# A feed-forward block with seven half-size products in place of eight, its weight sums split between GpSimd and adding transfers

## The reference, cut to what matters

```python
def gated_conv_ffn(x, w_gate, w_up, conv_w, conv_b, w_down):
    g = jnp.einsum('bsd,df->bsf', x, w_gate)
    g = causal_dwconv3(g, conv_w) + conv_b
    up = jnp.einsum('bsd,df->bsf', x, w_up)
    return jnp.einsum('bsf,fd->bsd', jax.nn.silu(g) * up, w_down)
# x = rms_norm(h, norm_ffn[layer]), in both layers; all in float32
```

## Time and profile before

| | us |
|---|---|
| three runs | 1753.5, 1754.58, 1755.64 (median 1754.58) |
| the profiled execution, from first to last instruction (span) | 1753.3 |
| PE busy | 1722.9 (98%) |
| DVE busy | 955.8 (55%) |
| ACT busy | 776.2 (44%) |
| POOL busy | 406.6 (23%) |
| chain that ended last, share of PE | 82% |

### The profile page before, as it was taken

The page is one execution under the profiler, slowest core; times in us unless marked ns, Lnnn a source line. Parts: engine busy times, 40 slices in busy tenths (PEclk is TensorE's granted clock), DMA queues, the critical chain, the costliest instruction groups (busy, mean ns, idle before and its releaser), DMA issues.

```text
span 1753.3 us, 25674 instructions
## 1 busy us (share of the span) xinstructions
PE 1722.9 (98%) x8611; PEld 1438.5 (82%) x8611; DVE 955.8 (55%) x1757; ACT 776.2 (44%) x1375; POOL 406.6 (23%) x545
## 2 busy tenths in 40 slices
PE   7999999999999999999999999999999999999998
PEld 7788889999878888888888888888788788888887
DVE  5677867777763334675555555333346555555332
ACT  6666766666652223432443333322364433333222
POOL 4555665655520001000211111011003211111000
PEclk9999999999999999999999999999999999999999
DMA  4112123333323334223233333333232333333332
GB/s 137 52 45 63 42 59 79 81 74 87 75 67 96 96 108 133 61 85 101 84 108 93 94 93 95 120 95 94 96 96 72 87 94 96 96 96 93 93 96 91
DMA packets 284314, 154.42 MB, mean 88 GB/s; under 512 B 12655, under 2 KB 278770, under 8 KB 284242
## 3 DMA queue, kind: packets, MB, share of 16 engines
q1 hardware_dynamic: 281714, 148.69, 29.4%
q0 software_dynamic: 2336, 4.47, 1.1%
q10 hardware_dynamic: 192, 0.33, 0.1%
HBM read 147.02 MB, written 2.16 MB: 85 GB/s over the span
## 4 chain that ended last, share of the span: by engine, by line
PE 82%; DVE 8%; issue 4%; ACT 4%; POOL 1%; DMA 0%; ACTq 0%; DVEq 0%; SPq 0%; POOLq 0%
PE ps L364 65%; PE ps L980 3%; PE ps L2505 2%; PE ps L830 2%; DVE tmp L1323 1%; DVE arena_r L1328 1%; PE ps L843 1%; PE ps L809 1%; ACT tmp L1051 1%; PE ps L788 1%; PE ps L1773 1%; ACT w_split L305 1%; PE ps L347 1%; PE ps L676 1%; DVE tmp L1380 1%
## 5 line engine op out<-in xcount | busy, mean ns | idle before, releaser
L364 PE MATMUL ps<-u,w_split 128*128 128x512 f32 x3705 | 876.9, 394 | 0.0
L364 PEld LDWEIGHTS ps<-u,w_split 128*128 128x128 f32 x3705 | 690.8, 188 | 152.1 <-issue 1.4
L321 DVE TENSOR_TENSOR w_split<-w_raw,w_split 128x1024 fp32r<-128x1024 f32 (+1 forms) x221 | 268.2, 1214 | 434.3 <-ACT w_split L305 434.2
L305 ACT CAST w_split<-w_raw 128x1024 fp32r<-128x1024 f32 (+4 forms) x321 | 289.0, 914 | 412.3 <-PE ps L364 376.6
L364 PE MATMUL ps<-arena_r,w_split 128*128 128x512 f32 x1758 | 402.0, 389 | 1.8 <-POOL w_split L319 1.5
L364 PEld LDWEIGHTS ps<-arena_r,w_split 128*128 128x128 f32 x1758 | 329.5, 188 | 72.2 <-POOL w_split L319 1.9
L2425 POOL TENSOR_TENSOR tmp<-tmp 128x512 f32<-128x512 f32 x44 | 57.1, 1298 | 422.1 <-ACT tmp L2410 422.1
L319 POOL TENSOR_TENSOR w_split<-w_raw,w_split 128x256 fp32r<-128x256 f32 x168 | 122.9, 763 | 23.7 <-ACT w_split L305 23.7
L980 PE MATMUL ps<-u,w_split 128*128 128x264 f32 x768 | 105.8, 287 | 2.0 <-DVE arena_r L1348 1.8
L1921 POOL TENSOR_TENSOR tmp<-tmp 128x512 f32<-128x512 f32 x33 | 46.8, 1417 | 261.1 <-ACT tmp L1877 232.4
L1051 ACT ACTIVATE tmp<-ps,stats 128x144 f32<-128x144 f32 (+3 forms) x128 | 69.4, 542 | 75.1 <-DVE stats L1315 73.0
(11 more groups left out here) (283 smaller groups left out, 1701.1 us busy)
## 6 DMA issues: line engine op xcount, KB each, us to landing
w_raw<-in_w_in_dram SPq DMA_DIRECT2D x118, 256.0 KB, 3.1
w_raw<-in_w_ffn_gate_dram SPq DMA_DIRECT2D x88, 256.0 KB, 3.1
w_raw<-in_w_ffn_up_dram SPq DMA_DIRECT2D x88, 256.0 KB, 3.2
w_raw<-in_w_ffn_down_dram SPq DMA_DIRECT2D x64, 256.0 KB, 3.1
w_raw<-in_w_in_even_dram SPq DMA_DIRECT2D x32, 256.0 KB, 3.0
w_raw<-in_w_in_odd_dram SPq DMA_DIRECT2D x32, 256.0 KB, 3.1
w_raw<-in_w_ffn_down_dram SPq DMA_DIRECT2D x32, 192.0 KB, 2.7
w_raw<-in_w_br_mla_dram SPq DMA_DIRECT2D x16, 256.0 KB, 3.1
```

The lines of the kernel that those rows point to most:

```text
L305: ins = act.copy(dst, src)
L321: ins = eng.tensor_tensor(lo, r, hi, ALU.subtract)
L364: last = pe.matmul(out_ap, w_tile(c, ws, k - n0), moving(k, ms), start=start and n == 0, stop=stop and n == len(total) - 1, skip_group_che ...
```

## The change

The first two tiles of each FFN (`PLAIN = 2`) are made as before. For each of the other 20 tiles the pair `gate`, `up` is seen as one product of 2 x 2 blocks: the weights are g1, g2, u1, u2 (the even and the odd k-tiles of the gate panel and of the up panel; a "quarter" of 128 x 512 each), the input is B11, B12, B21, B22 (even or odd k-tiles, left or right 256 tokens). A scheme of the Strassen-Winograd kind needs seven products of 4 k-tiles x 3 passes x 256 columns in place of eight. It takes sums of weights, sums of inputs and sums of results:

- Weight sums, for every tile: `e = u1 + u2` (first, a POOL instruction), `u1 += g1` (third, a transfer from SBUF to SBUF with `accum_op=ALU.add`, which POOL begins), `g1 += e` (second, a POOL instruction, in place), `g2 += g1` (fourth, again an adding transfer).
- Low splits: of the seven weights of a tile the low parts of p5 and p7 are made by POOL (`POOL_LO`), the other five by DVE. ACT makes all seven high parts.
- Input: once a layer `x_tok` (the input with its gain and `rbc`) by DVE, four sums by POOL, seven high parts by ACT, seven low parts by DVE. The factor `rbc` disappears from the 20 tiles.
- Results: ACT copies the running sum out of PSUM three times a tile (`snap`), DVE adds three halves of 256 columns. Tap, silu and the product with `up` work on 512 columns as before, now partly in PSUM.

The products of one period stand in the order p1, p4, p3, p2, p6, p5, p7, where p4 and p3 belong to the tile of the period before (`OF_LAST`). High and low splits are made three products ahead, into four slots of a quarter each. Outside the FFN the diff renames semaphores (`pro_act` and the like) and moves the spatial weights' load, with no other change.

```diff
+SEVEN = ("p1", "p4", "p3", "p2", "p6", "p5", "p7")
+OF_LAST = (1, 2)
+POOL_LO = (5, 6)
+WEIGHT_OF = {"p1": "g1", "p2": "g2", "p3": "g2", "p4": "u2", "p5": "e", "p6": "g1", "p7": "u1"}
...
+        def pe_seventh(pe, layer, i, fs, pos):
+            kind, gs = SEVEN[pos], pair_of(fs, pos)
+            low_split(pe, layer, i, fs, pos)
...
+            elif kind in ("p4", "p3"):
+                out_ = bank(R_BANK + gs % 2, 0, HT) if kind == "p4" else bank(Q_BANK, 0, HT)
+                pe.wait_ge(sem("combined"), combined(layer, i, gs, "up_right"))
...
+            for kk in range(4):
+                for n, (ws, ms) in enumerate(PASSES):
+                    ins = pe.matmul(out_, split_slot(layer, fs, pos, ws)[:, kk * P:(kk + 1) * P], XS[kind][:, kk, ms, :],
...
+            ins.then_inc(sem("s_used"), 1)
...
+        def act_seventh(act, layer, i, fs, pos):
...
+            if kind in ("p1", "p2", "p4"):
+                loaded(act, layer, i, gs)
+            else:
+                if kind in ("p5", "p6"):
+                    act.wait_ge(sem("summed_w"), summed_to(layer, i, gs, 1 if kind == "p5" else 2))
+                else:
+                    act.wait_ge(sem("third_sum" if kind == "p7" else "fourth_sum"), added_to(layer, i, gs))
...
+            act.copy(split_slot(layer, fs, pos, HI), quarter(layer, gs, WEIGHT_OF[kind])).then_inc(sem("s_hi"), 1)
...
+            def first_sum(i, gs):
+                loaded(pool, layer, i, gs)
...
+                pool.tensor_tensor(quarter(layer, gs, "e"), quarter(layer, gs, "u1"), quarter(layer, gs, "u2"), ALU.add) \
+                    .then_inc(sem("summed_w"), 1)
+
+            def third_sum(i, gs):
+                pool.wait_ge(sem("summed_w"), summed_to(layer, i, gs, 1))
+                pool.dma_start(quarter(layer, gs, "u1"), quarter(layer, gs, "g1"), accum_op=ALU.add) \
+                    .then_inc(sem("third_sum"), 16)
+
+            def second_sum(i, gs):
+                low_split(pool, layer, i, gs, 0)
+                pool.wait_ge(sem("third_sum"), added_to(layer, i, gs))
+                dst = quarter(layer, gs, "g1")
+                pool.tensor_tensor(dst, dst, quarter(layer, gs, "e"), ALU.add).then_inc(sem("summed_w"), 1)
+
+            def fourth_sum(i, gs):
+                low_split(pool, layer, i, gs, 3)
+                pool.wait_ge(sem("summed_w"), summed_to(layer, i, gs, 2))
+                pool.dma_start(quarter(layer, gs, "g2"), quarter(layer, gs, "g1"), accum_op=ALU.add) \
+                    .then_inc(sem("fourth_sum"), 16)
...
+            def period(i, fs):
+                for pos in POOL_LO:
+                    seventh_low(pool, layer, i, fs, pos)
+                fourth_sum(i, fs)
+                if fs < FT - 1:
+                    first_sum(i, fs + 1)
+                    third_sum(i, fs + 1)
+                    second_sum(i, fs + 1)
```

The period of ACT (`begun`: the tile is one of the 20; `carried`: there is a tile before it):

```diff
+                if carried:
+                    snap(i, fs - 1, 3)
...
+                    hi_ahead(i, fs, 0)
...
+                    snap(i, fs, 1)
...
+                    hi_ahead(i, fs, 1)
+                    hi_ahead(i, fs, 2)
...
+                    hi_ahead(i, fs, 3)
...
+                    first_tap(i, fs - 1)
...
+                    hi_ahead(i, fs, 4)
+                    snap(i, fs, 2)
...
+                    pair_silu(i, fs - 1)
...
+                    hi_ahead(i, fs, 5)
+                    hi_ahead(i, fs, 6)
...
+                    hidden_hi(i, fs - 1)
```

And where the down product's first panels are loaded:

```diff
+            sp.wait_ge(sem("fourth_sum"), added_to(layer, 0, FT - 1))
...
+            w_load(sp, c0, panel(dram, 0, DOWN[0], 0))
+            low_split(sp, layer, 0, FT, 1)
+            low_split(sp, layer, 0, FT, 2)
+            w_load(sp, c0 + 1, panel(dram, 0, DOWN[1], DOWN[0]))
```

More of the change, by code:

```diff
@@ L203, in hybrid_blocks_kernel @@
         hid, at = view(tmp, at, 1, SEQ)
+        rbc_ffn, at = view(tmp, at, 1, SEQ)
         cpad, at = view(tmp, rest, 1, 516)
@@ L1838, in body @@
             def body(i, first, last):
+                if first and name in (("down", 0), ("down", 1)):
+                    down_first(sp, name[1], dram)
                 for j in range(2):
@@ new lines, in per_tile, with used, loaded, low_split @@
+        def per_tile(layer, i, fs, back=0):
+            return num(FT * layer + fs + 1 - back, i, 4)
+        def used(layer, i, fs, pos):
+            return num(N_PROD * layer + NTH[fs, pos] + 1, i, 28)
+        def loaded(eng, layer, i, gs):
+            eng.wait_ge(sem(f"pair_load{gs % 2}"), num(64 * (N_PAIR // 2 * layer + (gs - PLAIN) // 2 + 1), i, 128))
+        def low_split(eng, layer, i, fs, pos):
+            mine = [a_ for a_ in ORDER if (a_[1] in POOL_LO) == (pos in POOL_LO)]
+            per = sum((p in POOL_LO) == (pos in POOL_LO) for p in range(7))
+            eng.wait_ge(sem("s_lo_pool" if pos in POOL_LO else "s_lo"),
+                        num(len(mine) * layer + mine.index((fs, pos)) + 1, i, 4 * per))
@@ L2358, in load_ffn @@
         def load_ffn(sp, layer):
             c0 = FIRST[("ffn", layer)]
-            def body(i, first, last):
-                for j in range(4):
-                    w = a["w_ffn_gate_2" if j % 2 == 0 else "w_ffn_up_2"][layer]
-                    w_load(sp, c0 + j, panel(w, (2 * i + j // 2) * P), i, 4)
-            loop(sp, FT // 2, body)
+            for f in range(PLAIN):
+                for j in range(2):
+                    w_load(sp, c0 + 2 * f + j, panel(a["w_ffn_up_2" if j else "w_ffn_gate_2"][layer], f * P))
@@ L2419, in pool_ffn, with at_tile @@
+            periods(act, period)
+        def at_tile(eng, i, gs):
+            return gs if isinstance(i, int) else 4 * i + gs
         def pool_ffn(pool, layer, tag):
             pool.wait_ge(sem("rbc"), norms_done(tag))
-            def body(i, first, last):
-                for j in range(2):
-                    pool.wait_ge(sem("ffn_silu"), FT * layer + 2 * i + j + 1)
-                    pool.tensor_tensor(cnv[:, j, :], cnv[:, j, :], rbc[:, 0, :], ALU.mult) \
-                        .then_inc(sem("ffn_scaled"), 1)
@@ L2429, in dve_ffn, with period @@
+            scaled(1)
+            pool_x(pool, layer, 2)
+            pool_x(pool, layer, 3)
+            def period(i, fs):
+                for pos in POOL_LO:
[5 more added lines that the diff above has]
+                    second_sum(i, fs + 1)
+            for fs in range(PLAIN, FT):
+                period(0, fs)
         def dve_ffn(dve, layer, tag):
```

607 lines of the change are left out of this document (455 added, 152 removed).

## The result

The changed kernel takes **1839.07 us** (median of 4 runs, 1838.01 to 1839.96) against 1755.11 (1753.5 to 1756.17) for the kernel before on the same chip: ratio 1.0475, 95% interval [1.046, 1.049]. Two terms of the sum were wrong in opposite directions, so that it came so close is luck; most of what follows is about these two.

What follows compares the result with a forecast made beforehand. POOL's chain of sums, splits and transfers was taken to bound the FFN at 12.8 us a period, above PE's 10.1. Span 1753.3 + 70 (periods) + 23 (FFN starts and ends) = 1846.7, median 1848 us; range 1757 to 1945.

Steps and rivals of the forecast that it cites:

- PE's side: FFN period on PE: 84 matmuls of 0.120 us, 10.1 us instead of 11.04, saving 37 us if PE stays the bound.
- The ring of POOL: POOL's sums, low parts and hops each FFN period: 7.48 + T + 0.3 = 12.8 us, +70 us.
- T: Time from an adding transfer's issue to its landing, estimated at 3.04 + 0.9 + 1.1 = 5.0 us.
- ring A: POOL's cycle through the third sum's transfer, second sum, low parts, fourth sum's issue and first sum; forecast 12.8 us.
- The second ring: From the fourth sum's issue through p3's high part, third snap, p4, p3 and p7's splits: T + 7.4 us.
- Contention in the ring: POOL's additions stretched where they meet DVE's work on SBUF: 0.3 us a period, bounds 0 and 0.6.
- The stall: PE idle some 2.7 us a period before p4, waiting for DVE's `combined`, with little before p6.
- The boundaries: PE waits at each FFN's start (9 us) and before the down product (2.5): 11.5 a layer, +23 us.
- The end: Before the down product PE waits some 2.5 us, its first panel being loaded only after the last fourth sum.
- Rival 2: Adding transfers land fast, 2.6 us, and PE stays the FFN's bound: 1741 us; chance 0.07.
- Rival 3: Adding transfers much slower than copies, landing in 6.5 to 9.4 us: 1948 at 7.5, 2024 at 9.4; chance 0.09.
- Rival 4: PE's clock falls in the stalls, p4 and p3 taking 5.8 us in place of 2.9: 1948 us; chance 0.07.

Runs made afterwards that it cites:

- lodve_snap_rbanks: Changed kernel with the low parts of p5 and p7 moved from POOL to DVE, third snap earlier, four PSUM banks for R products: 1785.74 us, ratio 1.0175.
- both_pool: Changed kernel with the third and fourth weight sums as POOL additions in place of adding transfers: 1838.22 us, ratio 1.0468.
- no_xsums: Changed kernel without POOL's four sums of the input blocks, plain blocks split in their place: 1826.89 us, ratio 1.041.
- copies: Changed kernel with its two adding transfers made plain copies of the same size, leaving out the third and fourth sums: 1791.4 us, ratio 1.0203.
- both_rbanks: Changed kernel with both transfers replaced by POOL additions and four PSUM banks in place of two for R products: 1866.65 us, ratio 1.0652.

## Why the prediction was right, point by point

- **PE's side** was right. The fastest single periods, in `lodve_snap_rbanks`, are 10.02 us long (10.1 forecast). The 37 us of PE time were there, but no version held that period: the best mean is 10.54.
- **The ring of POOL** was right in its mechanism. With the measured T of 3.8 its formula, 7.48 + T + 0.3, gives 11.6; ring A closes in about 11.5. The second ring, T + 7.4 with its own T of 4.7, gives 12.1; measured 11.9. "As long as the first" was right, and it is the second that binds, by a little.
- **T was the mis-sized term** of the steady part: 5.0 forecast, 3.8 and 4.7 measured. The base was too long (the quiet copy's 3.04 plus 0.9 for a neighbour; a copy in that place takes 2.3 and 3.0), the extra for adding too short (1.1; measured 1.5 and 1.7). The term came to +35 in place of +70.
- **Contention in the ring**, 0.3: the first sum takes 1.59 in place of 1.30, the second 1.27. Right. What was missed is that DVE pays far more than POOL; only `both_pool` made it decide.
- **The stall**, 2.7 us before p4: measured 0.90 there and 0.51 before p1, behind `hidden`, a wait the forecast did not name. The forecast took it as the period less PE's work, 12.8 - 10.1; by the same sum the measured period leaves 11.9 - 10.1 = 1.8, in two pieces. The rows give 1.4 for them, since idle time in a row begins at the end of a long matmul row and not when the next could have started.
- **The boundaries** were the other mis-sized term, +49 in place of +23. The step that failed is "PE would have its four plain products and the first five of the seven done at 22.8 + 7.2 = 30": it let PE run ahead until p7. (Two terms here are also above what they are added up from: four plain products are 96 starts of 0.230, 22.1 and not 22.8, and POOL's list from 20.5 on comes to 35.6 and not 37.7. Neither is what went wrong.) In fact PE stood 4.55 us within the plain products and 3.57 before p1, since DVE's list feeds these too and not only p7; then 10.27 before p6. DVE's part ran longer than its count because POOL's sums, which were counted at 2.47 and took 3.31, stretched it (2.88 for 0.69), shown by `no_xsums`. Behind these gaps the clock stood at half, which made PE's own work there 6.3 us longer. The end, 2.5, was 3.36 and a p4 at half clock, with another cause than the down product's load: the last p3's high part stands behind the fourth sum.
- **Rival 2** (transfers fast, PE the bound, 1741) would have been wrong in its time even where its condition holds: `copies` has a third sum landing in 2.3 us and takes 1791. The steady part does gain there, 40 x (11.04 - 10.61) = 17 us, but the boundaries cost 53, not 23. So with transfers that land as fast as these copies the change is still slower. **Rival 3** (T of 6.5 and more) did not occur. **Rival 4** (clock) did not occur in the periods, occurred at the starts, and is what made `both_rbanks` slow.
- The forecast was 35 us too high in the steady part and 26 too low at the boundaries, which left 9. The direction and the ring are the forecast's merit; that the time came within 9 us is luck.

What stays open: how the remaining 19 us or so of each start and end split between DVE's count of work and the plain tiles' order, and how much of the 6.3 us of half clock would come back if PE did not stand there; a version with less DVE work there was not built.

## What to carry to other kernels

Before an engine's work is cut, draw every ring of semaphores that returns to it, in its own units, with the latency of each transfer and hop in it: here PE's work in a period fell from 11.04 to 10.1 us, and the rings through the adding transfers and GpSimd's splits took 11.9. When two rings are within a few tenths, undoing one part alone shows nothing; open them one after another. And count each stage's start and end apart from its period: what a longer loop hides is exposed there, and here it was worth more than the steady part.

## What the runs showed that was not expected

- An adding transfer of 256 KB within SBUF lands after 3.8 to 4.7 us where a copy lands after 2.3 to 3.0, takes 0.88 us to issue in place of 0.57, and takes 1.64 us of each DMA engine in place of 0.77.
- A low part of 128x512 on DVE took 0.69 us alone, 1.15 in the median of `both_pool`, where POOL adds most of the time, and 2.88 beside POOL's addition of 128x1024 at an FFN's start. POOL's own work of 128x512 was stretched less, from 1.29 to 1.59 in the period shown and to 2.24 at the first start (906.01 in the changed kernel, beside DVE's input low part of 128x1024).
- The clock fell within a steady loop of PE that stood only 1.8 us a period (`both_rbanks`), and it did not in one that stood 1.70 (`both_pool`) or 0.5 and 0.9 (the changed kernel); in `fourth_pool` it fell behind a stall of 1.94 and not behind one of 2.05. Opening one wait, which only moved the stall from p1 to p4, thus made the kernel 1.5% slower (1866.65 against 1838.22).
